# Forming the weight of a sparse-attention probability row per head instead of per pair of heads

## The reference, cut to what matters

```python
p2 = jax.nn.softmax(s2 ...)                  # branch 1, selected blocks
o_slc = einsum('btgrnj,btgnjd->btgrd', p2, vg)
p = jax.nn.softmax(where(m, s, NEG))         # branch 2, sliding window
o = einsum('btgrs,bsgd->btgrd', p, v)
...
o_nsa = jnp.sum(o_nsa3 * pr['n_g'][..., None], axis=-2)
```

## Time and profile before

| what | value |
|---|---|
| median of three runs | 2023.07 us (2022.23 to 2031.38) |
| profiled execution | 2036.84 us, its span 2035.1 us |
| PE busy | 1842.7 us, 91% of the span |
| PEld busy | 1468.4 us, 72% |
| DVE busy | 889.4 us, 44% |
| POOL busy | 534.4 us, 26% |
| ACT busy | 520.7 us, 26% |
| L1258, exponentials, x128 | 67.3 us busy, 78.4 us idle before |
| L1268, weighted rows, x128 | 64.8 us busy, 67.0 us idle before, released by L1331 |
| L1205, transposes, x328 | 76.9 us busy, 53.9 us idle before |
| granted TensorE clock, mean | 0.916 of full speed |

### The profile page before, as it was taken

How to read it: one execution, slowest core, us unless ns; L and a number is a source line. 1 busy time by engine, 2 the same in 40 slices (tenths; PEclk the granted TensorE clock), 3 DMA queues, 4 the chain that set the end, 5 groups by cost and what they waited for, 6 DMA issues and landing times. The chain is left out here.

```text
span 2035.1 us, 25514 instructions
## 1 busy us (share of the span) xinstructions
PE 1842.7 (91%) x9456; PEld 1468.4 (72%) x9456; DVE 889.4 (44%) x1748; ACT 520.7 (26%) x1315; POOL 534.4 (26%) x718
## 2 busy tenths in 40 slices
PE   6999987678798999999999998876878999999998
PEld 5888765444477888888878886643545788888887
DVE  4016325874255434444320552368543544443433
ACT  2112233444422211111111123243434221110202
POOL 0007002746022221212300240047350322212223
PEclk7989888878589999999999898888885999999999
DMA  6411212446412222222241204045291212222223
GB/s 209 158 42 42 90 37 98 173 166 245 129 42 83 83 83 83 83 83 83 83 158 71 74 10 126 2 145 207 101 318 38 83 42 88 95 97 94 83 83 125
DMA packets 107931, 210.35 MB, mean 103 GB/s; under 512 B 28128, under 2 KB 37136, under 8 KB 103328
## 3 DMA queue, kind: packets, MB, share of 16 engines
q1 hardware_dynamic: 92944, 141.58, 21.0%
q0 software_dynamic: 13824, 67.12, 9.1%
q10 hardware_dynamic: 1040, 0.00, 0.0%
HBM read 200.00 MB, written 17.06 MB: 107 GB/s over the span
## 5 line engine op out<-in xcount | busy, mean ns | idle before, releaser
L524 PE MATMUL ps<-xt,ring 128*128 128x260 f32 x1536 | 355.9, 391 | 8.8 <-DVE xt L650 8.8
L524 PEld LDWEIGHTS ps<-xt,ring 128*128 128x128 f32 x1536 | 296.0, 195 | 56.4 <-issue 9.9
L2107 ACT ACTIVATE tt<-ps 128x260 f32<-128x260 f32 x108 | 41.8, 387 | 356.0 <-PE ps L2006 236.2
L2107 ACT ACTIVATE scr<-ps 128x260 f32<-128x260 f32 x108 | 41.8, 387 | 352.1 <-PE ps L2006 227.4
L1205 PE MATMUL ps<-cst,xt 128*128 128x128 f32 x328 | 76.9, 351 | 53.9 <-ACT xt L1268 42.1
L1205 PEld LDWEIGHTS ps<-cst,xt 128*128 128x128 f32 x328 | 45.4, 178 | 96.6 <-ACT xt L1268 66.4
L596 ACT ACTIVATE tt<-ps 128x520 f32<-128x520 f32 x48 | 28.9, 602 | 314.2 <-PE ps L524 314.2
L1346 DVE TENSOR_REDUCE small<-ps 128x1 f32<-128x512 f32 (+3 forms) x128 | 56.7, 484 | 99.9 <-PE ps L1190 99.8
L1814 POOL TENSOR_TENSOR tt<-ring,tt 128x1024 f32<-128x1024 f32 x32 | 82.5, 2592 | 48.9 <-DVE scr L1617 35.4
L2052 POOL TENSOR_TENSOR x_fm<-x_fm,scr 128x260 f32<-128x260 f32 x60 | 50.7, 844 | 162.4 <-DVE scr L2201 56.1
L724 POOL TENSOR_TENSOR big<-big,scr 128x128 f32<-128x128 f32 (+1 forms) x30 | 15.0, 499 | 294.9 <-DVE scr L677 293.4
(11 more groups left out here) (412 smaller groups left out, 3764.4 us busy)
## 6 DMA issues: line engine op xcount, KB each, us to landing
ring<-in_w_up SPq DMA_DIRECT2D x16, 2048.0 KB, 8.4
ring<-in_w_down SPq DMA_DIRECT2D x16, 2048.0 KB, 7.9
ring<-in_w_in SPq DMA_DIRECT2D x15, 2048.0 KB, 8.0
ring<-in_state_win_k SPq DMA_DIRECT2D x2, 2048.0 KB, 8.4
ring<-in_state_win_v SPq DMA_DIRECT2D x2, 2048.0 KB, 14.8
ring<-in_w_out SPq DMA_DIRECT2D x4, 1024.0 KB, 11.9
ring<-in_w_out SPq DMA_DIRECT2D x8, 512.0 KB, 16.3
out_s_win_k<-in_state_win_k SPq DMA_DIRECT2D x2, 2044.0 KB
```

The costliest lines, as they stand in the source:

```text
L524: ins = pe.matmul(self.ps[:, 2 * (u % 2) + half, 0:H], w[:, k, f * P:(f + 1) * P], self.xtv[:, k, half * H:(half + 1) * H], start=(k == 0) ...
L2107: act.activation(tmp(u, j), bank(u, 0), ACT.Copy).then_inc(done, 1)
```

## The change

The exponentials still count `exp_done` once per head. `norm` now waits for the first head's exponential, forms that head's weight on one column, and releases it; then it waits for the second head's, forms that weight on one column, and releases it. `w_ready` counts two per unit, ScalarE's scale of head g waits for its own count, and the branch-0 unit adds two at once.

```diff
@@ turn @@
-                pe.wait_ge(w_ready, w + 1)
+                pe.wait_ge(w_ready, 2 * w + 2)
@@ scale @@
-                act.wait_ge(w_ready, w + 1)
+                act.wait_ge(w_ready, 2 * w + g + 1)
@@ norm @@
-                dve.wait_ge(exp_done, 2 * w + 2)
                 if br == 0:
+                    dve.wait_ge(exp_done, 2 * w + 2)
...
-                    dve.tensor_tensor(pv, pv, wgt.unsqueeze(2).broadcast_to([P, 8, 16]), ALU.mult).then_inc(w_ready, 1)
+                    dve.tensor_tensor(pv, pv, wgt.unsqueeze(2).broadcast_to([P, 8, 16]), ALU.mult).then_inc(w_ready, 2)
                     return
                 k = slot(w, 0)
                 gate = own_gates[:, qt, :, br].rearrange("p (g r) -> p r g", g=2)[:, r]
-                link(dve.reciprocal(rcp[:, k:k + 2], rsum[:, k:k + 2]))
-                dve.tensor_tensor(rcp[:, k:k + 2], rcp[:, k:k + 2], gate, ALU.mult).then_inc(w_ready, 1)
+                for g in range(2):
+                    one = rcp[:, k + g:k + g + 1]
+                    dve.wait_ge(exp_done, 2 * w + g + 1)
+                    link(dve.reciprocal(one, rsum[:, k + g:k + g + 1]))
+                    dve.tensor_tensor(one, one, gate[:, g:g + 1], ALU.mult).then_inc(w_ready, 1)
```

## The result

| kernel | median | runs | ratio to before, 95% interval |
|---|---|---|---|
| before | 2025.68 us | 20 (2014.69 to 2031.80) | 1 |
| after | 2032.25 us | 20 (2024.49 to 2037.89) | 1.0033 (1.0019 to 1.0046) |

The forecast was +4.6 us, with this mechanism.

What follows compares the result with a forecast made beforehand. VectorE and GpSimd were taken to bound 355 to 432 us, the prompt job's loop of waits the tail. 1.57 + 1.0 - 0.26 = 2.3 us a layer, 4.6 in all: 2023.07 becomes 2027.7, said 2028 us; range 2020 to 2036.

Steps and rivals of the forecast that it cites:

- Step 357: Step at 357 us: second product waits for GpSimd's multiply, `largest` moves 2.19 us, less 0.62 us cover: 1.57 us.
- it reads from about 0.15 us after its recorded start: GpSimd's L1814 multiply takes hold of the port only about 0.15 us after its recorded start, inferred from one delayed L1814.
- the products at 377 and 398 us: Second products in two doubtful steps: taken to slip in ahead of GpSimd, costing nothing; if held, 0.7 us each at most.
- The rule of the Trainium skill: Two-SBUF-input VectorE and SBUF-reading GpSimd instructions exclude each other, the later blocked throughout; from recorded starts, 7.4 instead of 4.6 us.
- Step 419: Step at 419 us: second product held, `largest` moves about 2.3 us, less 1.56 us cover: 0.7 us on VectorE and GpSimd.
- the already held product at 438.91: Product inside GpSimd's L1834: held 0.7 us longer, second product adds 0.37 us, carried to L1516: 1.07, say 1.0 us.
- The last pair: Last pair of the tail, no scores behind it: head 0's earlier weight gains 0.26 us a layer.
- The tail: 524 to 564 us: L1268's 2.3 us of waits fall to near zero, loop's period unchanged, gain hidden by 0.63 us idling.
- The added instructions: One more reciprocal and product per pair, 0.37 us, where free of the port: costed at nothing; 6.7 us a layer uncovered.
- the third rival: VectorE has no cover from 355 to 432 us, each late pair pays 0.37 us: up to 2041 us; chance 0.18 beyond 0.5%.
- The second: Rival: the earlier weight counts, 4.6 us of tail waits come back, 2018.5 us; chance 0.05 within 0.5%, 0.04 beyond.
- The first: Rival: no second product is held, by slipping in ahead of GpSimd or other phases: 2022.6 us; chance 0.13.

Runs made afterwards that it cites:

- the five pairs alone: Against before: weights per head only in units 4, 6, 8, 10 and 17 of each layer, every other pair's one product counting one; 2032.29 us, ratio 1.0035.
- all others: Against before: weights per head in the 27 pairs of a layer other than units 4, 6, 8, 10, 17, whose product counts one; 2023.59 us, ratio 0.9993.
- a product of no use: Against before: both heads' weights together, counting one, then one more reciprocal and product on a spare column nobody reads; 2031.82 us, ratio 1.0030.
- after again: The changed kernel unaltered, a second profile of one execution; 2034.93 us, marks 134.09 and 130.70 us.
- 0.9998 above: The changed kernel with the gate as a scalar operand of the product (tensor_scalar instead of tensor_tensor); 2024.14 us, ratio 0.9998 to before.
- before again: The kernel before unaltered, a second profile of one execution; 2026.82 us, marks 130.26 and 130.32 us.

## Why the prediction came out as it did

**Sign and mechanism were right, the size in part by luck.** A second product that starts inside GpSimd's multiply stands still until its end, with `largest` and the sample pieces behind it. Three kernels whose counter steps by one show it from three sides: the five pairs alone bring the loss (1.0035), all others bring none that can be measured (0.9993), and a product of no use brings it as well (1.0030).

How the offsets of the first layer moved from before to after, from the starts of L1609, L1617, L1834 and L1516 (each minus its layer's first row maximum):

| place (time before) | shift after | step's share | predicted |
|---|---|---|---|
| L1609 of step 357 (359.83) | +1.48 us | +1.48 | +1.57 |
| first L1617 of step 377 (376.24) | +1.49 | 0 | 0 |
| L1617 behind the held product (381.07) | +2.26 | +0.77 | 0 taken, 0.7 if held |
| L1617 in step 398 (401.76) | +2.36 | +0.10 | 0 taken, 0.7 if held |
| L1617 in step 419 (422.12) | +2.95 | +0.59 | +0.7 |
| L1834 (438.39) | +2.96 | 0 | 0 |
| L1516 (444.44) | +3.19 | +0.23 | +0.37 |

- Step 357: +1.48 for 1.57. The cover of 0.62 us before L1609 is used up, as said. Right.
- **The step that failed: "it reads from about 0.15 us after its recorded start".** I took it from one L1814 that VectorE had delayed, and with it let the products at 377 and 398 us slip in. They don't. After, the second products start 0.09 us (379.08 beside 378.99) and 0.05 us (400.46 beside 400.41) after the multiply and are held to its end; the pair product above is held from 0.03 us. The nearest that pass start 0.04 to 0.05 us before it. So for these products the recorded starts decide, to within what these rows resolve. The rule of the Trainium skill that the prediction weighed ("SBUF — State Buffer", section "Who interferes with whom"), taken from recorded starts, was right about these two steps, and its 7.4 us lie inside the measured 3.8 to 9.3, as do my 4.6. The steps cost 0.77 and 0.10 us: the first the bound of 0.7, the second nearly hidden, since VectorE had waited 2.23 us for TensorE before the L1609 there (401.15 us in before).
- Step 419, right: +0.59 for 0.7. The prediction also said that VectorE finds slack behind it and GpSimd none: VectorE's sum of 431.40 is back at +2.33, L1834 stays at +2.96.
- **The place near 439 us failed as well: "the already held product at 438.91".** I took that hold as given, and it isn't, in before or in after. The first profile of before holds this product in both layers, the second in neither; there VectorE is through before GpSimd starts:

```profile
435.14 0.16 DVE L1331 TENSOR_TENSOR small<-small,gates 128x2 f32<-128x2 f32 x1
```

```profile
437.09 2.36 POOL L1834 TENSOR_TENSOR scr<-ring,pos_v 128x1024 f32<-128x1024 f32 x1
```

  In layer 1 of the first profile of after the product starts 0.01 us after L1837 and is held; in layer 2, and in both layers of its second profile, the pair is through before it. The two layers of the first profile, VectorE, then GpSimd:

```profile
441.14 2.35 DVE L1334 TENSOR_TENSOR small<-small,gates 128x1 f32<-128x1 f32 x1
...
1438.97 0.16 DVE L1334 TENSOR_TENSOR small<-small,gates 128x1 f32<-128x1 f32 x1
...
1439.23 0.16 DVE L1334 TENSOR_TENSOR small<-small,gates 128x1 f32<-128x1 f32 x1
```

```profile
441.13 2.34 POOL L1837 TENSOR_TENSOR scr<-ring,pos_v 128x1024 f32<-128x1024 f32 x1
...
1440.24 2.36 POOL L1837 TENSOR_TENSOR scr<-ring,pos_v 128x1024 f32<-128x1024 f32 x1
```

  The hold decides over 2.2 to 2.4 us at L1516, which starts 6.05 to 6.29 us after this multiply where the product is held and 3.84 to 3.86 us where it isn't. It doesn't decide the mark, which is 130.36 with the hold in before and 130.26 without; the clock in the last 10.4 us ahead of it was 0.84 and 0.50. So the path that I drew from 439 us through L1516 onward is not shown to reach the end of the stage. Over eight layers with the late products held (after, after again, the five pairs alone and the extra product, both counting one) the marks are 130.69 to 134.09 us, 132.53 in the mean, 2.2 us over before. Two layers make 4.4 us where I had 2 * 2.57 = 5.1; with two steps taken at nothing and a path that the clock cuts into, that they lie so near is luck.
- The last pair gained what was said. Timeline of after:

```profile
559.13 0.78 ACT L1268 ACTIVATE xt<-xt,small 128x128 f32<-128x128 f32 x2
559.60 0.84 PE L1205 MATMUL ps<-cst,xt 128*128 128x128 f32 x2 [0.17 <-ACT xt L1268]
```

  TensorE's 0.55 us of the earlier trace rows became 0.17, and from the last row maximum to the last L1309 copy it is 561.98 - 557.79 = 4.19 us, after 563.16 - 558.68 = 4.48 before: -0.29 for -0.26.
- The tail, right: L1268's 2.3 us of waits for a weight are gone there, and the loop is what it was: from the row maximum at 536.97 to the last at 558.68 it took 21.71 us before, 21.73 after (536.06 to 557.79). ScalarE's idling before the next exponential, 0.63 us in the earlier trace rows, is 0.93 us at 550.37: the 0.26 us went there.
- The added instructions cost nothing that can be measured where they are free (0.9993 and 0.9998 above): right, the third rival falls. The second falls with it, since an earlier weight alone brought nothing that can be measured. The first falls too: the holds of the steps near 357, 377, 398 and 419 us repeat in both profiles of after.

Counted from the marks, 4.4 - 2 * 0.29 gives 3.8 us, the lower end of the measured 3.8 to 9.3; the middle, 6.7 us, leaves some 3 us. Counted at L1834, ahead of the part in which the clock enters, the eight layers lie at 105.13 to 105.37 us and the six of before, before again and all other pairs per head counting one at 101.46 to 102.22: 3.4 us in the mean, 6.8 in two layers. That is near the middle, but that the end of the stage follows L1834 in full is not shown.

There are more held products behind the mark that I had not predicted: that of unit 17, near 139 to 143 us, in every layer of after, and in three of its four layers one or two near 150 and 156 to 159 us. These later ones are not needed for the loss. The five pairs alone have none there and cost as much (1.0035); all other pairs per head, counting one, have both in their second layer, and the part behind its mark takes 91.1 us, beside 92.2 in the layer without them. What the hold of unit 17 costs can't be read from profiles in which that part scatters by 7 us, and no run splits the other four pairs without it, so this stays open.

## What to carry to other kernels

Where one engine can be held by another's long operation, as VectorE here by GpSimd's multiplies, the count of added instructions matters less than where each starts against the long ones: ask of each added small operation which long operation of the neighbour was released by the same event, and in which hundredths of a microsecond the two start. Try a form of the operation that the neighbour does not hold before moving it, and look for the gain in the wait that the order of work makes (here 3.4 us in each of six late steps), not in the wait for the other half of an input. A point in the trace that repeats to a tenth of a microsecond in a few profiles can still hide two effects that cancel, here a late chain at a higher clock and an early one at the lower. A variant that is to isolate one part must change nothing else that is queued ahead of it: a counter stepping by two instead of one cost more than the change under study.

## What was not expected of the hardware

- Starts 0.05 us apart decide over 2.2 us. Products of two tensors that start with a multiply pass at 0.04 to 0.05 us before its start and are held from 0.01 us after it.
- In these kernels each product that adds two to its semaphore has its wait as a separate instruction; the 0.07 to 0.08 us that this takes, in five pairs a layer, cost 15 to 29 us (1.0073 to 1.0145).
- With the gate as a scalar operand the product takes 0.21 us instead of 0.16 and was not held in any of three profiles, 384 instructions, some of them starting 0.27 us inside a multiply.
- A hold can begin before the multiply's recorded start. In after, VectorE and then GpSimd:

```profile
494.84 2.82 DVE L1334 TENSOR_TENSOR small<-small,gates 128x1 f32<-128x1 f32 x1
```

```profile
494.31 0.94 POOL L282 DMA_INDIRECT ring<-in_cache_cmp_v,row_i  x1 [0.31 <-issue]
495.26 2.37 POOL L1837 TENSOR_TENSOR scr<-ring,pos_v 128x1024 f32<-128x1024 f32 x1
```

  The product starts inside the gather, 0.42 us before the multiply, and ends with the multiply, at 497.66 beside 497.63. Head 0's product passed in the same gather at 494.57. In the second profile of after the product at the same place, 0.56 us into the gather, passes. What decides there was not tried.
